# Feed-forward layer: sixteen gate and up pairs in seven products of quarter blocks instead of eight

## The reference

```python
x = x + y @ w_out
x = x + SwiGLU(RMSNorm(x))      # norm_ffn, w_gate_up (1024 x 5632), w_down (2816 x 1024)
y = RMSNorm(x)                  # norm_final
```

## Time and profile before

| | |
|---|---|
| median of the runs | 993.94 us |
| the profiled execution, its own time | 996.81 us |
| its span from the first to the last instruction | 995.0 us |
| TensorE busy | 967.9 us, 97% |
| VectorE busy | 507.7 us, 51% |
| ScalarE busy | 335.9 us, 34% |
| mean granted TensorE clock | 0.993 of full speed |

### The profile page before, as it was taken

The page is one execution under the profiler, slowest core; times in us unless marked ns, Lnnn a source line. Parts: engine busy times, 40 slices in busy tenths (PEclk is TensorE's granted clock), DMA queues, the critical chain, the costliest instruction groups (busy, mean ns, idle before and its releaser), DMA issues.

```text
span 995.0 us, 18231 instructions
## 1 busy us (share of the span) xinstructions
PE 967.9 (97%) x7611; PEld 945.0 (95%) x7611; DVE 507.7 (51%) x933; ACT 335.9 (34%) x559; POOL 77.6 (8%) x107
## 2 busy tenths in 40 slices
PE   6999999999999899999999999999999999999997
PEld 5899999999989889899999999999999999999997
DVE  5735556544887472635355565554445555333232
ACT  7344223444544350422222342222222222222222
POOL 0100013011210200111023000000000000000000
PEclk9899999999999999999999999999999999999999
DMA  7582326432320766122222345222222222222302
GB/s 240 153 262 42 48 77 95 156 108 77 98 65 1 218 192 200 43 86 85 86 86 85 127 147 189 85 88 92 99 96 95 86 85 75 85 75 80 111 1 91
DMA packets 104909, 104.77 MB, mean 105 GB/s; under 512 B 11130, under 2 KB 101752, under 8 KB 104492
## 3 DMA queue, kind: packets, MB, share of 16 engines
q1 hardware_dynamic: 101224, 92.51, 30.3%
q0 software_dynamic: 3552, 11.08, 3.7%
q10 hardware_dynamic: 52, 0.01, 0.0%
HBM read 97.74 MB, written 15.45 MB: 114 GB/s over the span
## 4 chain that ended last, share of the span: by engine, by line
PE 86%; SPq 3%; DVE 3%; ACT 2%; issue 2%; DMA 1%; POOL 1%; ACTq 0%; DVEq 0%; POOLq 0%
PE acc L466 74%; SPq L698 3%; PE acc L1168 1%; PE acc L1081 1%; POOL mt L854 1%; PE acc L1057 1%; PE acc L935 1%; PE acc L924 1%; PE acc L895 1%; PE acc L1041 1%; PE acc L1252 1%; ACT h_hi L1562 1%; DVE w_lo L449 0%; PE acc L1069 0%; DVE mt L1670 0%
## 5 line engine op out<-in xcount | busy, mean ns | idle before, releaser
L466 PE MATMUL acc<-h_hi,w_hi 128*128 128x256 f32 (+1 forms) x1520 | 462.0, 304 | 3.1 <-DVE w_lo L449 2.1
L466 PE MATMUL acc<-h_lo,w_hi 128*128 128x256 f32 (+1 forms) x1520 | 439.2, 289 | 0.0
L466 PE MATMUL acc<-h_hi,w_lo 128*128 128x256 f32 (+1 forms) x1504 | 433.0, 288 | 0.0
L466 PEld LDWEIGHTS acc<-h_hi,w_hi 128*128 128x128 f32 x1520 | 287.6, 189 | 12.0 <-issue 5.1
L466 PEld LDWEIGHTS acc<-h_lo,w_hi 128*128 128x128 f32 x1520 | 288.0, 189 | 4.1 <-issue 2.4
L439 ACT ACTIVATE w_hi<-raw 128x1024 fp32r<-128x1024 f32 (+1 forms) x135 | 140.9, 1043 | 444.9 <-PE acc L466 444.9
L466 PEld LDWEIGHTS acc<-h_hi,w_lo 128*128 128x128 f32 x1504 | 285.0, 189 | 0.0
L449 DVE TENSOR_TENSOR w_lo<-raw,w_hi 128x1024 fp32r<-128x1024 f32 (+1 forms) x134 | 164.0, 1224 | 107.6 <-ACT w_hi L439 102.9
L466 PE MATMUL acc<-s_hi,w_hi 128*128 128x256 f32 (+1 forms) x352 | 101.6, 288 | 0.0
L466 PE MATMUL acc<-s_lo,w_hi 128*128 128x256 f32 (+1 forms) x352 | 101.3, 288 | 0.0
L466 PE MATMUL acc<-s_hi,w_lo 128*128 128x256 f32 (+1 forms) x352 | 100.7, 286 | 0.0
(11 more groups left out here) (348 smaller groups left out, 1122.6 us busy)
## 6 DMA issues: line engine op xcount, KB each, us to landing
raw<-in_w_in SPq DMA_DIRECT2D x25, 1024.0 KB, 5.3
raw<-in_w_gate_up SPq DMA_DIRECT2D x22, 1024.0 KB, 4.9
raw<-in_w_down SPq DMA_DIRECT2D x8, 1024.0 KB, 4.7
rev<-tab POOLq DMA_DIRECT2D x1, 4352.0 KB, 19.4
ring<-in_cache_dsa_kv SPq DMA_DIRECT2D x4, 1024.0 KB, 7.3
raw<-in_w_out SPq DMA_DIRECT2D x4, 1024.0 KB, 5.1
out<-in_cache_dsa_kv SPq DMA_DIRECT2D x2, 2016.0 KB
ring<-in_cache_moba_k SPq DMA_DIRECT2D x48, 64.0 KB, 2.1
```

The costliest lines, as they stand in the source:

```text
L466: ins = nc.tensor.matmul(acc[:, bank, 0:HALF[half]], a[:, k, :], two(b[:, kx + k, :], half), start=first and k == k0 and c == 0, stop=last ...
```

## The change

Two blocks of 128 columns (one load) are now a pair. A pair's weights are seen as a two by two matrix of quarters: m is the block of output columns, k tiles are taken by twos (even and odd), and the tokens are two halves of 272. An ordinary product of such matrices takes eight products of quarters (`EIGHT_P`). Sixteen of the 22 gate and up pairs use a form with seven, which needs sums of quarters on both sides. A product is a chain of depth 4 (four k tiles; 3 for the last down chunk) by three matmuls, each with 272 columns. The moving side's sums (`h_parts`, `b_sum`) are formed once during the w_out stage: eight slots of 272 columns for each two k tiles, with high parts written by ScalarE and low parts by VectorE over 8 x 272 = 2176 columns at a time. The weight side's four sums (`w_sums`) are formed on VectorE for each pair. Operands (seven for such a pair, four for the others) go through a ring of six places of 128 x 512, high part on ScalarE, low part on VectorE. Partial sums are shared between results: ScalarE copies a bank into another, on which TensorE goes on accumulating (`bank_seeds`). The last two products of a seven-product pair, 4 and 3, are held until the next pair has begun; product 4 waits until result "22" has been taken out of its bank, which product 7 completed.

Gate and up are worked in three chunks of 4, 4 and 3 pairs, and the down pairs of a chunk follow the first gate pair of the next chunk. `xT` is multiplied by the root of the mean square (`over_rms`) so that the down results, which are not scaled by `rstd`, add up to it; the final norm takes that out again with `rtok`, for which `second_norm` has five small matmuls more.

```diff
+        KPS = (4, 4, 3)
+        FIRST = (0, 4, 8)
+        EIGHT = (0, 4, 8, 13, 17, 21)
...
+        SPLIT = (0, NPAIR - KD // 2)
+        EIGHT_P = [(m_, h, half) for m_ in range(2) for h in range(2) for half in (1, 2)]
+        stream, held = [], []
+        for n in range(NPAIR):
+            d = depth(n)
+            if n in seven:
+                stream += [(n, 1, 0, d)] + held + [(n, p, 0, d) for p in ((6, 5, 7, 2) if held else (5, 6, 2, 7))]
+                held = [(n, 4, 0, d), (n, 3, 0, d)]
+            else:
+                parts = [(0, d - 1), (d - 1, d)] if n in SPLIT else [(0, d)]
+                mine = [(n, p) + part for part in parts for p in EIGHT_P]
+                stream += mine[:2] + held + mine[2:]
+                held = []
...
+        RING, LEAD = 6, 5
...
+            return n_wout + 0.25 * i
...
+            return tm(last_use[operands[u - RING]] + 1) if u >= RING else tm(u - LEAD) if u >= 4 else n_wout - 0.94 + 0.05 * u
...
+                    yield tm(2)
+                    pe.wait_ge(sem("ssq_done"), KD)
                     for half in range(2):
...
+                    for i in range(NT + 1):
+                        n = P if i < NT else TS
+                        ins = nc.tensor.matmul(acc[0:n, OLD[4], 300 + i:301 + i], ssq[:, P * i:P * i + n], ones[:, 0:1], start=True, stop=True,
+                                               skip_group_check=True)
...
+                        if p == 4:
+                            pe.wait_ge(ffn_ev, evacs[n, "22"])
...
+                        for z, (a, b) in enumerate(((hi, b_his), (hi, b_los), (lo, b_his))):
+                            ins = nc.tensor.matmul(bank(n, name), a[:, k, :], b[:, k, slot, :], start=opens and k == k0 and z == 0,
+                                                   stop=closes and k == k1 - 1 and z == 2, skip_group_check=True)
...
+                        nc.scalar.activation(w_slot(u, False), w_source(n, p), ACT.Copy).then_inc(w_hi_done, 1)
...
+                        nc.scalar.copy(dst, src).then_inc(seeded, 1)
...
                         if half == 1:
-                            dve.wait_ge(sem("h2_hi_done"), k + 1)
-                            nc.vector.scalar_tensor_tensor(h_lo[:, k, :], xT[:, k, :], vecs[:, 8 + k:9 + k],
-                                                           h_hi[:, k, :].bitcast(F32), ALU.mult, ALU.subtract).then_inc(sem("h2_lo_done"), 1)
-                            add_squares(k, "sq2_done", "ssq2_done")
...
+                            add_squares(k, 0)
...
+                    for q in range(3):
+                        yield n_merge + 2 * q + 2.2
+                        dve.wait_ge(sem("hs_done"), 2 * q + 2)
+                        b_sum(4, 1, 0, "b_sum")
+                        b_sum(6, 2, 0, "b_sum")
+                        dve.wait_ge(sem("b_sum"), 4 * q + 1)
+                        b_sum(5, 2, 4, "b_sum")
+                        dve.wait_ge(sem("b_sum"), 4 * q + 3)
+                        b_sum(7, 5, 3, "b_sum")
+                        yield n_merge + 2 * q + 2.7
+                        dve.wait_ge(b_hi, 2 * KD + q + 1)
+                        b_low(slice(0, 8), h8_hi[:, q], h8_lo[:, q])
...
+                        nc.vector.tensor_tensor(*terms, ALU.add).then_inc(sem("w_sum"), 1)
...
+                        nc.vector.tensor_tensor(w_slot(u, True), w_source(n, p), w_slot(u, False).bitcast(F32),
+                                                ALU.subtract).then_inc(w_lo_done, 1)
...
+                    for k in range(KD):
+                        yield tm(8.5 + 2 * k)
+                        v.do(nc.vector.tensor_tensor(xT[:, k, :], xT[:, k, :], ssq[:, :], ALU.mult))
```

More of the change, by code:

```diff
@@ L187, in build @@
         xT = keep("xT", [P, KD, T])
+        h_at = keep.at
         h_hi = keep("h_hi", [P, KD, T], F32R)
@@ L355, in build @@
         n_wout = len(blocks)
[L356 to L364, removed]
+        n_all = n_wout
+        ffn_load = len(loads)
@@ new lines, in build, with gate_or_up @@
+        KPS = (4, 4, 3)
+        FIRST = (0, 4, 8)
+        EIGHT = (0, 4, 8, 13, 17, 21)
+        pairs, seven = [], set()
+        def gate_or_up(kind, c, j):
+            if sum(p[0] != "down" for p in pairs) not in EIGHT:
+                seven.add(len(pairs))
+            pairs.append((kind, c, j))
+        for c in range(len(KPS)):
+            for m_ in range(KPS[c]):
+                gate_or_up("gate", c, FIRST[c] + m_)
+                if m_ == 0 and c > 0:
+                    pairs += [("down", c - 1, j) for j in range(KD // 2)]
+                gate_or_up("up", c, FIRST[c] + m_)
@@ new lines, in build, with depth @@
+        pairs += [("down", len(KPS) - 1, j) for j in range(KD // 2)]
+        NPAIR = len(pairs)
+        for kind, c, j in pairs:
+            if kind == "down":
+                k0 = 2 * FIRST[c]
+                loads.append(([(0, 0, rows(w_dn, k0, k0 + 2 * KPS[c], 2 * j * P, 256))], 2 * P))
+            else:
+                loads.append(([(0, 0, rows(w_gu, 0, KD, (D_FF if kind == "up" else 0) + 2 * j * P, 256))], 2 * P))
+        def depth(n):
+            return KPS[pairs[n][1]] if pairs[n][0] == "down" else KD // 2
@@ L397, in build @@
                         g.append(allot(w) + (True, True, half, k0, k1))
-            elif w < n_gu:
+            else:
                 for half in range(2):
                     g.append(allot(w) + (True, True, half, 0, KD))
[L401 to L406, removed]
             groups.append(g)
@@ new lines, in build @@
+        evac_time = {(n, name): t for _, t, n, name in results_at}
+        copies = []
+        for i, (n, p, k0, k1) in enumerate(stream):
+            if n in seven and p in (1, 5, 6):
+                copies.append((i, n, {1: "b", 5: "p5", 6: "c"}[p]))
+                if p == (5 if pos[n, 6] < pos[n, 5] else 6):
+                    copies.append((i, n, "u2"))
+        seeds = {(n, what): i + 1 for i, (_, n, what) in enumerate(copies)}
+        halves = {n: i + 1 for i, n in enumerate(sorted(seven))}
```

501 lines of the change are left out of this document (393 added, 108 removed).

## The result

The changed kernel takes 1006.76 us (median of 4 runs, 1005.97 to 1008.18), the kernel before 993.6 beside it: ratio 1.0138, 95% interval 1.0113 to 1.0164. The prediction was 987.6, and its range ended at 1001. The profiled execution took 1006.62 with a span of 1004.5, so 9.8 us more than the one of before (the medians differ by 13.2: the profiled execution of before lay 3 us above its median).

A forecast was written before the change was run, and what follows sets the result against it. TensorE's matmuls were taken to set the time; -24.1 + 1.5 + 1.6 + 4.8 + 1.25 + 5.5 + 2.5 + 0.6 = -6.35 us, from a median of 993.9 to 987.6 us, range 974 to 1001.

The forecast's parts named there:

- rival D: Seven-product pairs: VectorE sets the pace, 11.6 us a pair against TensorE's 10.55, giving 1003 us; chance 0.17.
- steady part: Seven-product pairs: VectorE's 10.1 us fits under TensorE's 10.55, so little is lost: +1.5 us, bounded by 0 and 17.
- Matmuls: Sixteen gate and up pairs in seven products save 192 matmuls on TensorE: -24.1 us.
- Rival C: No change: five places with one product between 7 and 4 each lose 1.2 us, giving 993.6 us; chance 0.18.
- head pause: Start of the feed-forward layer: TensorE waits for the second norm's sum of squares, +4.8 us (2 to 7).
- Pair 1: First seven-product pair: product 4 waits for result "22" behind VectorE's late work, +5.5 us (1 to 8).
- five small matmuls: Second norm: five more one-column matmuls, about 1.0 us, and two that open banks, together +1.25 us.
- Clock: TensorE's lower clock after the two pauses at the layer's head and pair 1: +2.5 us for both (0 to 6.8).
- w_out: Stage before the feed-forward layer: chained operand sums make the fifth and seventh block late, +1.6 us (0 to 3).
- tail: End of the kernel: the last two results leave VectorE later, behind a sum of squares, +0.6 us (0 to 1.2).

The follow-up runs named there:

- e8: e7 with 20 of 22 gate and up pairs in seven products in place of 16: 978.3 us.
- e9: Changed kernel with only the two casts of an up pair's gated products put behind the copy for product 7 on ScalarE: 997.4 us.
- e1: Changed kernel with the copy for product 7 put ahead of both casts and sigmoids on ScalarE: 995.3 us.
- e2: Changed kernel with the second norm taken after product 7 of pair 0 instead of after product 2, root and reciprocal following later: 1006.0 us.
- e10: Changed kernel with only the two sigmoids of a gate pair put behind the copy for product 7 on ScalarE: 1005.4 us.
- e12: Changed kernel with the edits of e1 and e2 together: 989.7 us.
- e3: Changed kernel with all 22 gate and up pairs in eight products, none in seven: 1006.9 us.
- e5: e12 with the gated products 0.6 us earlier in VectorE's order: 983.9 us.
- e7: e12 with the gated products earlier and the multiplications by the norm's reciprocal spread to one in 6 us: 981.5 us.

## Why the prediction was wrong

The direction was wrong, and the time 19 us off. The range itself was too short for what the prediction held possible: its rival D stands at 1003, beyond the end at 1001, and the bounds of the terms, added straight, give 974 to 999 without the 17 of the steady part and 1014 with it, not 980 to 996.

- **Matmuls, -24.1: right.** 84 of 272 columns at 0.125 us, 192 fewer.
- **The steady part, +1.5 predicted, 17.2 measured: the step that failed.** "So VectorE fits, with 4% to spare, if in order and without gaps" held, in e8 up to 95% full. But then only product 4 and result "22" were followed through the queues. Product 7 waits for a copy on ScalarE, and ScalarE was judged by its sum, 6 us of 10.55. Busy for 171 of the layer's 412 us, it still held TensorE eleven times, because the copy stood behind casts and sigmoids that wait for VectorE. The order of ScalarE was there to be read in the changed kernel: 1.5, 1.75 and 1.8 stand ahead of 2.0. e9 shows the cause on its own: ScalarE's order alone gives 9.4 us back. The bound of 17 that I kept for this term was right in size and assigned to another mechanism (D), which e8 refutes: that it fits the 17.2 is luck. Rival C looked at the wrong places too: of its five places for a pause at product 4 only that in pair 1 ever shows one over 0.1 us (3.68 us in e1), and the three waits of 1.48 us in e1 stand in pairs that follow a seven-product pair, where it saw 3.0 us of slack.
- **The head pause, +4.8 predicted, 4.44 measured: right.** The chain was added up well: block 8's second addition leaves VectorE 4.7 us after the layer's start (5.0 predicted), the sum of squares 6.8 (7.1). But taking it away alone gains nearly nothing (e2): the pause only moves.
- **Pair 1, +5.5 predicted, 2.64 measured,** and not for the result "22" but for the seed of product 6, which stood behind the sigmoids at 608.56 (they end at 609.76, the copy at 610.05, and product 6 starts at 610.15; with the sigmoids later, in e10, it does not wait). The backlog that was predicted is real: it shows as 3.68 us at product 4 in e1, where ScalarE no longer holds TensorE first, and, beside the copy's place on ScalarE, in the 7.11 of e2.
- **The five small matmuls, +1.25 predicted:** the norm takes 1.94 us where it is not held up (e12), 1.0 more than before: the five were right. Behind the pause it took 3.8: it was priced at full clock and ran at half.
- **Clock, +2.5 predicted, 10.2 measured.** The argument that a second pause absorbs the loss of the first was wrong: the half clock ran for 10.2 us around the first (587.3 to 597.5, 5.1 us lost), and came back behind three later pauses, two of them in the steady part, of which the prediction had none. The earlier trace rows had the drop right in kind. The table of the Trainium skill, TensorE: Matmul & The Clock Gate, § Why this matters for your kernels, warns of idle gaps between bursts. The drop at the pause of 4.44 us agrees with it; the other three followed pauses of 2.64, 1.95 and 1.95 us, shorter than the gaps it names, and four more of 1.95 had none, and there the measurement decides.
- **w_out, +1.6 predicted, 1.0 measured** (0.55 and 0.41 at the fifth and seventh block): right in place.
- **The tail, +0.6 predicted, -1.9 measured.** The last result is not late on the path: 1.03 us from the first tail matmul to the transposes in both. In the changed kernel TensorE keeps its clock over the tail (first row), where it was 0.50 from 984 to 987 before, and the 36 transposes behind the small matmuls take 4.15 us and not 5.82 (second and third row):

```profile
992.00:1004.00 12.00, 7.09 (x65) 6.67 (x63) 4.84 (x13) 4.91 (x8) 0.00 (x0) 0.99 0.48 187
...
983.60 5.82 PE L1252 MATMUL acc<-con,xT 128*128 128x128 f32 x36
...
994.95 4.15 PE L1481 MATMUL acc<-con,xT 128*128 128x128 f32 x36
```

But that is not where the 1.9 us went. e1, e3, e5 and e9 have the new tail with a drop at the same place (e3: 5.80 us for the 36 transposes) and take 12.4 to 12.5 us, so the clock is worth 0.3 to 0.4. The other 1.5 lie behind the last store: issued 9.23 us after the first tail matmul in before and in e1 alike, it lands 4.3 us later in before and 2.7 in e1 (first and second row). Only one profile shows the 4.3, and its cause stays open.

```profile
out<-o_st SPq DMA_DIRECT2D x1, 128.0 KB, 4.3
...
out<-o_st SPq DMA_DIRECT2D x1, 128.0 KB, 2.7
```

By the terms: -24.1 + 17.2 + 4.6 + 2.8 + 10.2 + 1.0 + 1.1 left over = 12.8 for the layer (12.9 measured), -1.9 for the tail, and a start 1.5 us earlier: the 9.5 us between the two spans (995.0 and 1004.5).

## What to carry to other kernels

Summing up an engine's work tells only whether it can be the bound. For every operand that the critical engine waits for, walk the queue of the engine that makes it, even one that is 42% full: what stands ahead, and for whom does that wait. Put the short instruction that frees the critical engine ahead of those that wait for a third engine, then see what is late next (here three rounds: ScalarE's copies, the gated product, VectorE's backlog), because the repairs of the copies and of the head pause each showed or grew a wait that had been covered.

## What the runs showed of the hardware

- The half clock's length varied much. After a pause of 4.44 us it ran until 597.5, ten us in all; after 1.95 us twice for some 3.4 us (781.9 to 785.3, 829.7 to 833.1) and four times not at all; after 2.60 us in e7 there was a drop, after the same 2.60 us at the same product in e8 none (1.00 in each stretch of 2 us from 604 to 610). What decides it stays open: no run isolates it.
- A copy from accumulator to accumulator of 128 x 272 on ScalarE takes 0.38 us as shown and lets the next instruction start after 0.32 (625.78 to 626.10).
- In the tail, behind the same 1.03 us between the last product and the transposes, the clock fell in before, e1, e3, e5 and e9 and kept its level in the changed kernel and the other seven runs. No run was aimed at it.
